# A two-block transformer kernel on one core: every modulation column is summed on TensorE, and the later columns move from the first projections into the attention slots

## The chip, the cores and the metric

The kernel runs on one core of a Trainium2 chip, as one program. The metric is the device time of the whole program in microseconds. Times of a run are given as a median over several executions; the profile is of one further execution.

## What is computed

Two transformer blocks follow each other on a sequence of 512 tokens with 1024 channels, in 32-bit floats. What matters here is the start of the first block:

```
cond = silu(c)
mod  = cond @ ada_w + ada_b                      # 6 x 1024 values
shift1, scale1, gate1, shift2, scale2, gate2 = mod
u    = rmsnorm(x, norm_mix) * (1 + scale1) + shift1
aq, ak, av, bq, bkv, biq, bik, biw, cq, ck, cv, g = split(u @ w_in)
merged = sigmoid(g) parts * (diff_attention @ w_br_a, dsa_attention @ w_br_b, moba_attention @ w_br_c)
x    = x + gate1 * (merged @ w_o)
u2   = rmsnorm(x, norm_mlp) * (1 + scale2) + shift2
x    = x + gate2 * (square(relu(u2 @ w_ff1)) @ w_ff2)
```

`mod` is a row vector times a 1024 x 6144 matrix. The kernel holds it as 48 columns of 128 values (`modc[:, m]`): columns 0 to 15 are shift1 and scale1, 16 to 23 gate1, 24 to 39 shift2 and scale2, 40 to 47 gate2. The second block (a convolution and state-space mixer, gated linear attention, two cross attentions, two more feed-forward parts) takes most of the time and isn't touched.

## The kernel before, in words

**Units and slots.** Nearly all work with weights is cut into units. `plan` (L203) makes them and puts them in one fixed order. A unit is 128 output columns of a weight matrix: a 1024 x 128 block, 512 KB (`Unit`, L173). Every engine walks through the same order of units with its own function, and semaphores join them. SyncE (`sync_program`, L635) issues one transfer per unit into a ring of five slots (`RAW_SLOTS`, w0 to w4); before the transfer of unit n it waits until unit n - 5 has been used up (L644 to L655). A projection unit is split: ScalarE rounds the block to its high part (`round_ahead`, L1230, instruction L1239), VectorE or, for some units, GpSimd takes the low part (`lower_ahead`, L1796 and L2556), and TensorE makes 24 matmuls of 512 columns (`products`, L690, instructions L699, L701, L703). Both look up to four units or two split units ahead. "Slots" of an attention are the places at which each engine runs a few units between the scores of one tile and the rows of the tile before it. An attention has 16 tiles (4 heads x 4 query tiles) and 17 slots.

**Modulation units.** A modulation unit (name "ada") isn't split. Before the change there are two ways to use it. On VectorE (`ada_sum`, L1899): multiply the first 128-row chunk by its cond values (L1906), then multiply and add seven more (L1909), into one of two tiles `adat`; then TensorE adds over the partitions with one matmul against a column of ones (L740 in the opening, `ada_total` L721 and instruction L725 later), and VectorE adds the bias (L1915). On TensorE (`ada_first`, L729): eight matmuls, each with a 128 x 128 chunk as the stationary operand and one column of cond as the moving one (L737); the profile counts each 32-bit matmul as two instructions, so 16 for a unit.

**Order of the work around the change.**
- Opening (up to about 90 us): transposes of the input, then 12 "flips" for the bias tables (`flip_over`, L825, instruction L829; their operands come by GpSimd's transfers of 256 KB each, L2621, four ahead), with modulation units 0 to 15 between them: four ahead of head 1, then one for each head ahead of the flip of the head before. Even units go by VectorE, odd ones by TensorE. Then the first norm (`modulated`, L1986 and L1425) makes the inputs XH and XL.
- First projections (`plans["project"]`, 12 units): av, aq, ak. From the fourth on each is followed by a modulation unit (16 to 24), on VectorE.
- Differential attention, 17 slots: 15 projection units (cv, bq, kv, iq, ik, iw, cq, ck) and 17 modulation units (25 to 41), on VectorE. At the end of each head come the weighted values (`weigh`, L862, instruction L865) after ScalarE's copy of the transposed rows (L1228 in `rows_turned`, L1443), and a norm (L781).
- Index scores, 6 slots, and moba attention, 17 slots: gate and branch units only; the 48 selection rounds of VectorE (L2118, L2120) stand in moba's slots.
- Latent attention ("dsa"), 17 slots: gate and branch units, and modulation units 42 to 47 in the first six, with a last step "ada end".
- Then branch b, w_o, the feed-forward part, and the second block.

A few lines say how slots are filled before the change:

```
plans["project"] = project[:3]
for u in project[3:]:
    plans["project"] += [u, next(rest)]
for i in range(17):
    plans["diff", i] = [u for u in (next(fill, None), next(rest)) if u]
for i in range(6):
    plans["index", i] = [next(fill)]
```

## Time and profile before

| | |
|---|---|
| median of 3 runs | 3233.36 us (3229.53 to 3238.36) |
| the profiled execution, its own time | 3232.45 us |
| its span in the trace | 3230.7 us |
| busy: TensorE matmul, weight load | 2762.0 us (85%), 2164.7 us (67%) |
| busy: VectorE, ScalarE, GpSimd | 1678.0 us (52%), 1059.7 us (33%), 473.8 us (15%) |
| chain that ended last | TensorE 65%, VectorE 23%, ScalarE 7%, transfers 2% |
| VectorE, L1909 (sums of modulation units) | 280 instructions, 115.9 us, mean 414 ns |
| modulation weights | 48 transfers of 512 KB, 4.8 us to landing |

PE is TensorE's matmuls, PEld its weight loads, DVE VectorE, ACT ScalarE, POOL GpSimd, SP SyncE. Times count from the start of the span. "L699" is line 699 of the kernel. In a row of waits the engine and line that waited stand first, then what released it. A granted clock of 1.00 is 2.4 GHz and of 0.50 is 1.2 GHz. "ps" is an accumulator bank, "w_f" a weight slot, "modc" the modulation columns, "wh" and "w_r" high and low parts of a unit.

### The profile page before, as it was taken

The numbers are of one execution on the slowest core, as the hardware profiler recorded it, in microseconds if no ns is written. First come the engines' busy times: TensorE is split into PE (matmuls) and PEld (weight loads), VectorE is DVE, ScalarE is ACT, GpSimd is POOL, SyncE is SP. The second block draws the span as 40 slices with busy tenths as digits, with TensorE's granted clock in tenths as the row PEclk, the third lists the DMA queues.
The fourth block names the chain that finished last, engine by engine and source line by source line (L and its number), as shares of the span: only waits on it lengthen the run. The fifth ranks groups of instructions, "written<-read, shape, count | busy, mean of one in ns | idle before, by whom it ended". The sixth has DMA issues, their size and how long they took to land.

```text
span 3230.7 us, 29906 instructions
## 1 busy us (share of the span) xinstructions
PE 2762.0 (85%) x11897; PEld 2164.7 (67%) x11897; DVE 1678.0 (52%) x2474; ACT 1059.7 (33%) x1670; POOL 473.8 (15%) x344
## 2 busy tenths in 40 slices
PE   6879596889999987855669998999889899989996
PEld 5656364667888865644547866888657778668885
DVE  3466567545433259878865445332463373453324
ACT  2223342433332121221243434332343244343322
POOL 1021131320000024222311001000100030110001
PEclk6887797999999988977789999999999999999998
DMA  6442221222333321200023312333222033223331
GB/s 197 113 111 73 59 65 31 79 83 80 98 91 98 92 65 52 72 13 13 20 66 104 105 56 74 92 98 91 73 65 66 27 111 98 65 73 92 98 92 59
DMA packets 481275, 251.07 MB, mean 78 GB/s; under 512 B 13534, under 2 KB 478002, under 8 KB 481135
## 3 DMA queue, kind: packets, MB, share of 16 engines
q1 hardware_dynamic: 478516, 242.43, 26.3%
q0 software_dynamic: 1904, 5.73, 0.6%
q8 instruction: 93, 1.52, 0.2%
q10 hardware_dynamic: 715, 1.01, 0.1%
q14 instruction: 47, 0.39, 0.0%
HBM read 247.00 MB, written 2.13 MB: 77 GB/s over the span
## 4 chain that ended last, share of the span: by engine, by line
PE 65%; DVE 23%; ACT 7%; issue 2%; DMA 2%; POOL 0%; SPq 0%; DVEq 0%; ACTq 0%; POOLq 0%
PE ps L701 18%; PE ps L703 18%; PE ps L699 18%; DVE arena_f L2213 6%; DVE adat L1909 2%; DMA w_f<-in_w_in 2%; PE ps L865 1%; ACT wh L1239 1%; PE ps L1108 1%; PE ps L781 1%; DVE arena_f L1871 1%; ACT arena_f L1441 1%; DVE hT L2343 1%; DVE arena_f L1868 1%; ACT hT L1679 1%
## 5 line engine op out<-in xcount | busy, mean ns | idle before, releaser
L699 PE MATMUL ps<-XH,wh 128*128 128x512 f32 x2160 | 887.7, 411 | 81.8 <-ACT wh L1239 27.9
L703 PE MATMUL ps<-XH,w_r 128*128 128x512 f32 x2160 | 873.1, 404 | 21.5 <-POOL w_r L2556 12.2
L701 PE MATMUL ps<-XL,wh 128*128 128x512 f32 x1968 | 800.8, 407 | 3.9 <-DVE XL L1801 3.9
L1796 DVE TENSOR_TENSOR w_r<-w_f,wh 128x1024 fp32r<-128x1024 f32 x336 | 411.0, 1226 | 575.1 <-ACT wh L1239 575.0
L699 PEld LDWEIGHTS ps<-XH,wh 128*128 128x128 f32 x2160 | 421.9, 195 | 206.4 <-ACT XH L1665 30.2
L1239 ACT ACTIVATE wh<-w_f 128x1024 fp32r<-128x1024 f32 (+2 forms) x423 | 428.2, 1016 | 389.8 <-PE ps L703 310.7
L703 PEld LDWEIGHTS ps<-XH,w_r 128*128 128x128 f32 x2160 | 418.3, 194 | 127.4 <-POOL w_r L2556 18.7
L701 PE MATMUL ps<-arena_r,wh 128*128 128x512 f32 (+1 forms) x1280 | 479.9, 375 | 0.0
L701 PEld LDWEIGHTS ps<-XL,wh 128*128 128x128 f32 x1968 | 383.8, 195 | 97.6 <-DVE XL L1801 7.3
L699 PE MATMUL ps<-arena_r,wh 128*128 128x512 f32 (+1 forms) x944 | 351.9, 373 | 5.8 <-DVE hT L1844 3.1
L703 PE MATMUL ps<-arena_r,w_r 128*128 128x512 f32 (+1 forms) x944 | 345.7, 366 | 6.8 <-DVE w_r L1796 6.7
L2556 POOL TENSOR_TENSOR w_r<-w_f,wh 128x1024 fp32r<-128x1024 f32 (+3 forms) x87 | 187.8, 2163 | 791.3 <-ACT wh L1239 791.0
L701 PEld LDWEIGHTS ps<-arena_r,wh 128*128 128x128 f32 x1280 | 243.4, 190 | 45.4 <-issue 1.9
L2213 DVE SCALAR_TENSOR_TENSOR arena_f<-arena_f,vec 128x512 f32<-128x512 f32 x240 | 210.1, 875 | 8.5
L699 PEld LDWEIGHTS ps<-arena_r,wh 128*128 128x128 f32 x944 | 180.5, 191 | 44.2 <-issue 5.4
L703 PEld LDWEIGHTS ps<-arena_r,w_r 128*128 128x128 f32 x944 | 180.3, 191 | 37.9 <-DVE w_r L1796 8.1
L1228 ACT ACTIVATE arena_f<-ps 128x512 f32<-128x512 f32 (+4 forms) x188 | 87.5, 482 | 203.5 <-PE ps L703 97.9
L1325 ACT ACTIVATE arena_f<-ps 128x512 f32<-128x512 f32 x96 | 57.3, 597 | 275.0 <-PE ps L703 274.9
L2593 POOL TENSOR_TENSOR arena_f<-arena_f 128x512 f32<-128x512 f32 x48 | 50.0, 1042 | 554.3 <-ACT arena_f L1325 554.3
L1909 DVE SCALAR_TENSOR_TENSOR adat<-w_f,modc,adat 128x128 f32<-128x128 f32 x280 | 115.9, 414 | 9.9
L1272 ACT ACTIVATE sq<-hT 128x512 f32<-128x512 f32 x63 | 39.7, 632 | 213.5 <-DVE hT L1844 160.2
L1801 DVE TENSOR_TENSOR arena_r<-arena_f,arena_r 128x512 fp32r<-128x512 f32 x66 | 45.7, 693 | 119.4 <-ACT arena_r L1362 111.1
(302 smaller groups left out, 2838.6 us busy)
## 6 DMA issues: line engine op xcount, KB each, us to landing
w_f<-in_mlp_w SPq DMA_DIRECT2D x128, 512.0 KB, 3.9
w_f<-in_w_ff SPq DMA_DIRECT2D x64, 512.0 KB, 3.9
w_f<-in_w_in SPq DMA_DIRECT2D x49, 512.0 KB, 3.8
w_f<-in_ada_w SPq DMA_DIRECT2D x48, 512.0 KB, 4.8
w_f<-in_even_w_in SPq DMA_DIRECT2D x36, 512.0 KB, 3.8
w_f<-in_odd_w_in SPq DMA_DIRECT2D x24, 512.0 KB, 3.8
w_f<-in_even_w_out SPq DMA_DIRECT2D x16, 512.0 KB, 3.7
w_f<-in_xa_w_v SPq DMA_DIRECT2D x16, 512.0 KB, 3.5
```

The costliest lines, as they stand in the source:

```text
L699: e.matmul(b, hi[:, k, :], xh, start=u.first and k == 0, stop=False)
L701: e.matmul(b, hi[:, k, :], xl, start=False, stop=False)
L703: last = e.matmul(b, lo[:, k, :], xh, start=False, stop=u.final and k == u.kc - 1)
L1228: return e.activation(o, i, ACT.Copy, scale=scale).then_inc(act.sem, act.up(*mark))
L1239: e.activation(high_flat(u), flat(u, 0), ACT.Copy).then_inc(act.sem, act.up("high", u.n))
L1325: e.activation(ffn_h[:, m, :], b, ACT.Relu).then_inc(act.sem, act.up("ff relu", st, m))
L1796: e.tensor_tensor(flat(u, 1), flat(u, 0), high_flat(u).bitcast(F32), ALU.subtract).then_inc(dve.sem, dve.up("low", u.n))
L1801: e.tensor_tensor(o, i, high.bitcast(F32), ALU.subtract).then_inc(dve.sem, dve.up("xl", source, k))
L1909: e.scalar_tensor_tensor(out=a, in0=wt[:, k, :], scalar=cond[:, k, :], in1=a, op0=ALU.mult, op1=ALU.add).then_inc(dve.sem, dve.up("ada sum ...
L2213: e.scalar_tensor_tensor(out=o, in0=val[:, m, t:t + S], scalar=conv_tap(t, m), in1=o, op0=ALU.mult, op1=ALU.add).then_inc(dve.sem, dve.up())
L2556: e.tensor_tensor(flat(u, 1), flat(u, 0), high_flat(u).bitcast(F32), ALU.subtract).then_inc(pool.sem, pool.up("low", u.n))
L2593: e.tensor_tensor(ffn_h[:, m, :], ffn_h[:, m, :], ffn_h[:, m, :], ALU.mult).then_inc(pool.sem, pool.up("ffn", name[1], m))
```

## The change

All 48 modulation units are used on TensorE, by eight matmuls each. The VectorE sums, the two tiles `adat` and the products with ones are gone. In the opening TensorE writes columns 0 to 15 into one bank as before. For the later columns (`ada_block`) TensorE takes a bank of the attention's ring, and ScalarE adds the bias and writes the column. The first projections have no modulation units; the differential attention has units 16 to 32 in its 17 slots, the index scores 33 to 38 in 6, and the latent attention 39 to 47 in its first nine. SyncE's wait for a slot is always for TensorE. The diff:

```diff
--- before.py
+++ after.py
@@ -209,9 +209,7 @@
 
     project = (columns_of("av", w_in, COL_AV, 512, "X0", lead=True) + columns_of("aq", w_in, COL_AQ, 512, "X0")
                + columns_of("ak", w_in, COL_AK, 512, "X0"))
-    plans["project"] = project[:3]
-    for u in project[3:]:
-        plans["project"] += [u, next(rest)]
+    plans["project"] = project
 
     ik = Unit("ik", 0, [w_in[:, COL_IK:COL_IK + IDX_DIM]] * 4, "X0")
     iw = Unit("iw", 0, [w_in[:, COL_IW:COL_IW + 8]], "X0")
@@ -231,11 +229,10 @@
 
     fill = iter(branch(0, A["w_br_a"][0], "ya"))
     for i in range(6):
-        plans["index", i] = [next(fill)]
+        plans["index", i] = [next(fill), next(rest)]
     for i in range(17):
         plans["moba", i] = [u for u in (next(fill, None),) if u]
     fill = iter(branch(2, A["w_br_c"][0], "yc"))
-    rest = iter([*rest, Step("ada end")])
     for i in range(17):
         plans["dsa", i] = [u for u in (next(fill, None), next(rest, None)) if u]
     plans["branch b"] = branch(1, A["w_br_b"][0], "yb")
@@ -348,7 +345,6 @@
         XH = sb("XH", [P, KC, S], F32R)
         XL = sb("XL", [P, KC, S], F32R)
         high_slots = [sb(f"wh{i}", [P, KC, WC], F32R) for i in range(HIGH_SLOTS)]
-        adat = sb("adat", [P, 2, P])
 
         def two_views(name, words):
             start = -(-nc.sbuf_base // 32) * 32
@@ -409,7 +405,6 @@
             before = sq_rings[st] = Ring(f"sq {st}", [sq[:, 0, :], sq[:, 1, :]], rings, after=before)
         gate_ring = Ring("gates", [gates[:, j, :] for j in range(2)], rings)
         st_ring = Ring("soft", [soft[:, 4 * j:4 * j + 4] for j in range(8)], rings)
-        ada_ring = Ring("ada", [adat[:, j, :] for j in range(2)], rings)
 
 
         xin, o1 = area(0, NT, D)
@@ -644,10 +639,7 @@
             for u in units:
                 if u.n >= RAW_SLOTS:
                     old = units[u.n - RAW_SLOTS]
-                    if old.name == "ada" and not (old.m < 16 and old.m % 2):
-                        w.wait_ge(dve, "ada sum", old.m)
-                    else:
-                        w.wait_ge(pe, "unit", old.n)
+                    w.wait_ge(pe, "unit", old.n)
                 c = 0
                 for d in u.dram:
                     dst = chunks(raw_slots[u.raw][0], u.kc, u.cols)[:, :, c:c + d.shape[1]]
@@ -718,28 +710,19 @@
                         last = e.matmul(b[:, t * 8:t * 8 + 8], xh, lo[:, k, :], start=False, stop=k == KC - 1)
                 last.then_inc(pe.sem, pe.up("unit", u.n))
 
-            def ada_total(m):
-                b, freed = att_now[0].take("ada", m)
-                w.wait_ge(*freed)
-                w.wait_ge(dve, "ada sum", m)
-                e.matmul(b[:, 0:1], ada_ring.of(m), ones[:, 0:1], start=True, stop=True).then_inc(
-                    pe.sem, pe.up("ada", m))
-                ada_ring.free(pe, m)
-
-            def ada_first(u, b):
-
-                if u.m % 2 == 0:
-                    return
+            def ada_column(u, b):
+
                 wt = chunks(flat(u, 0), KC, P)
                 w.wait_ge(d_raw[u.raw], "unit", u.n)
                 w.wait_ge(dve, "cond")
                 for k in range(KC):
-                    last = e.matmul(b[:, u.m:u.m + 1], wt[:, k, :], cond[:, k, :], start=k == 0, stop=k == KC - 1)
+                    last = e.matmul(b, wt[:, k, :], cond[:, k, :], start=k == 0, stop=k == KC - 1)
                 last.then_inc(pe.sem, pe.up("unit", u.n))
-                w.wait_ge(dve, "ada sum", u.m - 1)
-                e.matmul(b[:, u.m - 1:u.m], ada_ring.of(u.m - 1), ones[:, 0:1], start=True, stop=True).then_inc(
-                    pe.sem, pe.up("ada", u.m - 1))
-                ada_ring.free(pe, u.m - 1)
+
+            def ada_block(u):
+                b, freed = att_now[0].take("ada", u.m)
+                w.wait_ge(*freed)
+                ada_column(u, b[:, 0:1])
 
             def memory_turn(li, k):
                 b, freed = att_now[0].take("mem", li, k)
@@ -756,13 +739,9 @@
                 while steps:
                     u = steps.pop(0)
                     if isinstance(u, Step):
-                        if u.name == "ada end":
-                            ada_total(47)
-                        else:
-                            memory_turn(u.name[1], u.m)
+                        memory_turn(u.name[1], u.m)
                     elif u.name == "ada":
-                        if u.m > 16:
-                            ada_total(u.m - 1)
+                        ada_block(u)
                     elif u.name == "iw":
                         index_weights(u)
                     else:
@@ -833,11 +812,13 @@
             w.wait_ge(*freed)
             for h in range(12):
                 for _ in range(4 if h == 0 else 1):
-                    ada_first(next(first), ada_bank)
+                    u = next(first)
+                    ada_column(u, ada_bank[:, u.m:u.m + 1])
                 if h:
                     flip_over(h - 1)
             flip_over(11)
-            ada_first(next(first), ada_bank)
+            u = next(first)
+            ada_column(u, ada_bank[:, u.m:u.m + 1])
             run("project")
             flush()
 
@@ -1289,7 +1270,15 @@
 
             def evacuate(u):
                 name, m = u.name, u.m
-                if not u.final or name in ("ada", "iw"):
+                if not u.final or name == "iw":
+                    return
+                if name == "ada":
+                    b = att_now[0].of("ada", m)
+                    w.wait_ge(pe, "unit", u.n)
+                    w.wait_ge(dve, "vec", 0)
+                    e.activation(modc[:, m:m + 1], b[:, 0:1], ACT.Identity, bias=column("ada_b", m)).then_inc(
+                        act.sem, act.up("mod", m))
+                    att_now[0].free(act, "ada", m)
                     return
                 b = lin.of(*u.out)[:, 0:u.tokens]
                 if name in copied:
@@ -1373,8 +1362,7 @@
                 while steps:
                     u = steps.pop(0)
                     if isinstance(u, Step):
-                        if u.name != "ada end":
-                            memory_part(u.name[1], u.m)
+                        memory_part(u.name[1], u.m)
                         continue
                     round_ahead(u.n)
                     evacuate(u)
@@ -1812,7 +1800,9 @@
                 name, m = u.name, u.m
                 if not u.final:
                     return
-                b = None if name == "ada" else lin.of(*u.out)
+                if name == "ada":
+                    return
+                b = lin.of(*u.out)
                 if name == "iw":
                     w.wait_ge(pe, "unit", u.n)
                     e.tensor_scalar(iw, b[:, 0:32].rearrange("p (a b) -> p a b", a=NT),
@@ -1831,7 +1821,7 @@
                 elif name in RESIDUAL:
                     st = RESIDUAL[name]
                     w.wait_ge(pe, "unit", u.n)
-                    w.wait_ge(dve, "mod", 47)
+                    w.wait_ge(act, "mod", 23 if st == "r0" else 47)
                     e.scalar_tensor_tensor(out=hT[:, m, :], in0=b[:, :], scalar=gate(0 if st == "r0" else 1, m),
                                            in1=hT[:, m, :], op0=ALU.mult, op1=ALU.add).then_inc(dve.sem, dve.up("h", st, m))
                     lin.free(dve, *u.out)
@@ -1896,25 +1886,6 @@
                     e.scalar_tensor_tensor(out=go[:, m, :], in0=sca[:, m % 2, :], scalar=1.0, in1=go[:, m, :],
                                            op0=ALU.add, op1=ALU.mult).then_inc(dve.sem, dve.up("og", m))
 
-            def ada_sum(u):
-
-                a, freed = ada_ring.take(u.m)
-                wt = chunks(flat(u, 0), KC, P)
-                w.wait_ge(*freed)
-                w.wait_ge(d_raw[u.raw], "unit", u.n)
-                w.wait_ge(dve, "cond")
-                e.tensor_scalar(a, wt[:, 0, :], cond[:, 0, :], None, ALU.mult).then_inc(dve.sem, dve.up())
-                for k in range(1, KC):
-                    w.wait_ge(dve, dve.count)
-                    e.scalar_tensor_tensor(out=a, in0=wt[:, k, :], scalar=cond[:, k, :], in1=a, op0=ALU.mult, op1=ALU.add).then_inc(
-                        dve.sem, dve.up("ada sum", u.m))
-
-            def ada_total(m):
-                b = att_now[0].of("ada", m)
-                w.wait_ge(pe, "ada", m)
-                e.tensor_tensor(modc[:, m:m + 1], b[:, 0:1], column("ada_b", m), ALU.add).then_inc(dve.sem, dve.up("mod", m))
-                att_now[0].free(dve, "ada", m)
-
             def memory_part(li, k):
                 b = att_now[0].of("mem", li, k)
                 w.wait_ge(act, "xh", ("mem", li), k)
@@ -1929,20 +1900,12 @@
                 while steps:
                     u = steps.pop(0)
                     if isinstance(u, Step):
-                        if u.name == "ada end":
-                            ada_total(47)
-                        else:
-                            memory_part(u.name[1], u.m)
+                        memory_part(u.name[1], u.m)
                         continue
-                    if u.name == "ada" and u.m > 16:
-                        ada_total(u.m - 1)
                     lower_ahead(u.n)
-                    if u.name == "ada":
-                        ada_sum(u)
-                    else:
-                        evacuate(u)
-                        if u.pair:
-                            evacuate(steps.pop(0))
+                    evacuate(u)
+                    if u.pair:
+                        evacuate(steps.pop(0))
 
             def run(stage):
                 run_steps(plans[stage])
@@ -1969,14 +1932,8 @@
                 add_square("mix", k)
             e.memset(lamb[BUCKETS:BUCKETS + 1, 0:12], 1.0).then_inc(dve.sem, dve.up("table row"))
 
-            def ada_first(u):
+            for u in plans["ada first"]:
                 lower_ahead(u.n)
-                if u.m % 2 == 0:
-                    ada_sum(u)
-
-            for u in plans["ada first"]:
-                ada_first(u)
-            w.wait_ge(pe, "ada", 14)
             w.wait_ge(pe, *unit_mark("ada", 15))
             e.tensor_tensor(modc[:, 0:16], lin.of("ada first")[:, 0:16], columns("ada_b", 0, 16), ALU.add).then_inc(
                 dve.sem, dve.up("mod", 15))
@@ -1987,6 +1944,8 @@
                 s = modc[:, 24 * i + 8:24 * i + 16]
                 ring = sq_rings[f"n{i}"]
                 w.wait_ge(dve, dve.count)
+                if i:
+                    w.wait_ge(act, "mod", 39)
                 e.scalar_tensor_tensor(out=s, in0=s, scalar=1.0, in1=columns(name, 0, 8), op0=ALU.add, op1=ALU.mult).then_inc(
                     dve.sem, dve.up("gain", i))
```

## Rows read from the trace of the kernel before

**Rows 1.** The page: granted TensorE clock in 40 equal slices, in tenths
```profile
...
PEclk6887797999999988977789999999999999999998
...
```

**Rows 2.** Windows: start:end length, busy us PE PEld DVE ACT POOL, clock, DMA share, GB/s
```profile
...
41.90:72.80 30.90, 30.87 (x90) 21.60 (x91) 6.14 (x18) 4.84 (x9) 4.83 (x9) 0.50 0.80 241
...
121.40:183.80 62.40, 48.94 (x189) 37.77 (x187) 26.88 (x71) 11.71 (x15) 2.39 (x1) 0.89 0.44 118
183.80:396.50 212.70, 159.79 (x625) 114.96 (x624) 132.13 (x318) 75.17 (x146) 37.44 (x17) 0.79 0.30 80
396.50:440.50 44.00, 40.27 (x156) 25.66 (x156) 19.66 (x28) 16.94 (x33) 13.08 (x9) 0.91 0.15 42
...
547.30:600.00 52.70, 40.87 (x170) 30.89 (x169) 35.30 (x84) 15.47 (x35) 15.21 (x12) 0.93 0.31 86
...
```

**Rows 3.** TensorE in order of time, opening (start us, duration, line, count, [idle before])
```profile
...
31.70 3.57 PE L737 MATMUL ps<-modc,w_f 128*128 128x1 f32 x16
...
41.93 2.07 PE L829 MATMUL ps<-arena_f,const 128*128 128x512 f32 x2 [2.40 <-DMA arena_f<-strip]
...
47.50 3.76 PE L829 MATMUL ps<-arena_f,const 128*128 128x512 f32 x4
51.05 3.41 PE L737 MATMUL ps<-modc,w_f 128*128 128x1 f32 x16
54.32 0.56 PE L740 MATMUL ps<-ones,adat 128*128 128x1 f32 x2
...
83.78 1.87 PE L737 MATMUL ps<-modc,w_f 128*128 128x1 f32 x16
87.26 0.59 PE L740 MATMUL ps<-ones,adat 128*128 128x1 f32 x2 [1.60 <-DVE adat L1909]
```

**Rows 4.** Chain of waits inside the first projections (start us, us, what)
```profile
...
127.67 3.86 DMA w_f<-in_w_in
...
131.56 1.07 ACT wh L1239
...
132.72 1.23 DVE w_r L1796
...
136.95 4.01 DMA w_f<-in_w_in
...
```

**Rows 5.** TensorE in order of time, first projections: one unit without a wait
```profile
...
115.79 0.48 PE L699 MATMUL ps<-XH,wh 128*128 128x512 f32 x1
...
121.43 0.28 PE L725 MATMUL ps<-ones,adat 128*128 128x1 f32 x2
...
```

**Rows 6.** TensorE's waits, first projections from 121.4 us (total us, times, longest)
```profile
...
PE ps L725 <- DVE adat L1909: 13.5, 6, 3.5
```

**Rows 7.** TensorE's waits, differential attention, 183.8 to 396.5 us
```profile
...
PE ps L725 <- DVE adat L1909: 16.8, 5, 7.8
...
PE ps L865 <- ACT arena_f L1228: 10.7, 3, 6.0
PE ps L850 <- ACT arena_f L1252: 4.2, 1, 4.2
...
PE ps L850 <- DVE arena_f L2036: 3.4, 3, 1.4
PE ps L865 <- DVE modc L1915: 2.6, 1, 2.6
```

**Rows 8.** TensorE's waits, latent attention's slots with a modulation column, 547.3 to 600 us
```profile
PE ps L725 <- DVE adat L1909: 6.7, 3, 4.6
PE ps L865 <- ACT arena_f L1228: 5.1, 1, 5.1
```

**Rows 9.** Windows: an idle gap and behind it; 8-column matmuls (L716 to L718)
```profile
...
133.80:136.90 3.10, 0.00 (x0) 0.00 (x0) 2.85 (x10) 0.00 (x0) 0.00 (x0) 1.00 0.00 0
138.50:141.40 2.90, 2.90 (x8) 2.28 (x7) 0.00 (x0) 0.42 (x1) 0.00 (x0) 0.50 1.11 303
298.70:315.00 16.30, 16.30 (x80) 16.30 (x80) 7.46 (x18) 2.43 (x5) 3.79 (x2) 0.51 0.13 33
...
```

## The prediction

> **What bounds the kernel now.** I read the granted clock over the whole span first, then windows by stage, then TensorE's and the chain's own order of time in the stages that the change touches, then TensorE's waits there. The whole-span clock [rows 1] shows that TensorE is granted less than full speed in the first fifth of the span and nearly full speed after it; the change lies within the first 650 us. The windows [rows 2] show what limits each stage. In the opening TensorE is busy 30.87 of 30.90 us at 0.50 of full clock: it is the bound, at the lower level (1.2 GHz). In the first projections from 121.4 us it is busy 48.9 of 62.4 us. The chain inside that stage shows why [rows 4]: a weight load lands in 3.86 us, ScalarE rounds it (1.07), VectorE takes the low part (1.23), then sums a modulation unit, and only that sum frees the slot for which the next load waits, 9.28 us later (127.67 to 136.95). A projection unit needs 5.64 us of TensorE when nothing is late (115.79 to 121.43) [rows 5]. So VectorE's sum sits in the loop of the loads. In the differential attention TensorE is busy 159.8 of 212.7 us; in the index scores 40.3 of 44.0; in the part of the latent attention with modulation columns 40.9 of 52.7 [rows 2]. TensorE's waits say what the idle time is made of [rows 6 to 8].
>
> **The price of a unit on TensorE.** A modulation unit on TensorE is 16 matmuls of one column. At 0.50 of the clock they take 3.27 us from start to the next instruction (51.05 to 54.32); the last such unit took 1.87 us [rows 3]. In the opening I take 3.27. In the attention slots the price p runs from 1.87 (full clock, no loss) to 3.27 plus the clock that such work costs its neighbours. Rows of that: behind a 3.10 us gap TensorE ran 2.90 us at the lower level, which loses 1.45 us of work; and 100 matmuls of 8 columns held it near 0.51 for 16.3 us while it was busy throughout [rows 9]. So p lies between 1.87 and 3.27 + 1.45 = 4.72. I take 2.5, nearer the lower end: between two modulation units there stands a projection unit of 5.64 us, long enough to win the clock back as it did behind the gap; about four such losses in ten units give 1.87 + 0.6.
>
> **Opening, +17.8 us.** Removed: 8 VectorE sums and 8 products with the ones column. Added: 8 units on TensorE, 16 in all. Flip 0 now starts at 41.93, when its transfer lands. Ahead of it come five units instead of two: 31.70 + 5 x 3.27 = 48.1, so that transfer is no longer the wait. Behind it are 12 flips at 1.78 us (47.50 to 51.05 for two) and 11 units: 48.1 + 21.4 + 36.0 = 105.5. Now it ends at 87.26 + 0.59 = 87.85, its two last waits for VectorE included [rows 3]. Rounded with the small gaps: +17.8. It delays the shift and gain columns of the first norm, and with them everything. Nearest upper bound the same; lower bound below, as a rival. The first projection loads move later with it, since their slots are freed by TensorE, but each has four units of lead.
>
> **First projections, -22.3.** Nine modulation units with their loads, sums and ones products leave. The 62.4 us from 121.4 to the first scores [rows 2] become 7 x 5.64 + 0.6 for the last transposes = 40.1. The waits are 13.5 of that [rows 6]; most of the rest is lower clock behind them. It needs the loads to keep up: a load is ready 3.86 + 1.07 + 1.23 = 6.2 us after its slot is free [rows 4], with five slots of 5.64 us each. If only the waits went, it would be -13.5; that is the bound on the other side.
>
> **Differential attention, 17p - 34.** It keeps 17 modulation units (now 16 to 32). VectorE loses 17 sums; TensorE gains 17p. TensorE's waits that go: 16.8 for the sums, 4.2 and 3.4 ahead of scores, and 8.3 of the 13.3 ahead of the weighted values (L865), where ScalarE's copy was held behind a load whose slot a VectorE sum freed late; what stays there is ScalarE's own copy, an estimated 1.25 us at each of four heads [rows 7]. That is 32.7; the 17 ones products give 2.4 back, and the last slot, which has no projection, keeps 1. The other waits (norms) remain. With p = 2.5: +8.5.
>
> **Index scores, 6p = +15.** Units 33 to 38, with six 512 KB loads on SP's queue, go into a stage where TensorE is busy 92% and transfers take a 0.15 share [rows 2]. Nothing there can hide TensorE work. The selection rounds behind it start later by the same amount; they stand in slots and don't absorb it.
>
> **Latent attention, 9p - 11.3 = +11.2.** Nine units instead of six. Waits that go: 6.7, and 3.8 of 5.1 [rows 8]; six ones products, 0.8.
>
> **At nothing.** ScalarE gets 32 additions of one column. None is in the trace; the nearest ScalarE row shown takes 1.07 us for 1024 columns [rows 4]. So they lie between 0 and 34 us in all; I take about 0.2 us each, hidden, because ScalarE's next step in every slot is the copy of transposed rows that TensorE makes after the modulation unit anyway. GpSimd's queue is not touched. SP waits for TensorE in place of VectorE: loads three units ahead wait for the modulation unit of the slot before, which is done before that slot's successor begins. The residual's wait on the last columns is long satisfied.
>
> **Sum.** 17.8 - 22.3 + 32p - 34 - 11.3 = 32p - 49.8. With p = 2.5: +30.2. The profiled execution took 3232.45 us, 0.9 below the median of the three runs, so no correction is needed: 3263. With p = 1.87 it is +10.0, with 3.27 +54.8. A gain would need p under 1.56 us, less than the fastest unit in the trace.
>
> **Rivals.** (1) Faster: **one-column products run at full clock**. The opening shows the reverse, 0.50 through 30.9 us of work without a gap [rows 2]. It would be supported only by the last unit of the opening at 1.87. Then the fifth unit ends at 31.70 + 9.35 = 41.05, before flip 0's transfer; with flips at an estimated 0.9 the opening ends at 41.93 + 10.8 + 20.6 = 73.3, -14.6; slots at 1.87 give 32p = 59.8; and the 0.79 clock of the attention [rows 2] would rise, an estimated 16 us. Sum: -14.6 - 22.3 + 59.8 - 45.3 - 16 = -38, 3194 us. It decides from the point at which the alternation of flips and units is granted the upper level. The Trainium skill, "TensorE: Matmul & The Clock Gate", section "What's actually happening", says that the throttled state is the default and activity releases it; by that rule the extra matmuls would warm the engine, while the opening's row says that this kind of activity does not. Chance 0.06.
> (2) No change: the opening is slow, but in the slots the gaps that cost the clock go, and p is 1.87: +10 less up to 16, so -6 to +9, about 3234. For it: six of ten gaps are VectorE's. Against: each unit is itself like a gap to the clock, by the 8-column row [rows 9]. Chance 0.15.
> (3) Worse: modulation units and the short projection units behind them (index, latent) keep TensorE at the lower level, p = 3.27 + 0.8: +80, 3313; or ScalarE waits at each load since the ring of five slots now holds only two and a half slots' units. For it: 0.15 DMA share is little, so mostly the clock. Chance 0.11.
> My forecast, p between 1.9 and 3.3: 0.68.
>
> **How the numbers follow.** A measurement of this kernel tells about 0.3%, 9.7 us, from no change. Forecast and rival 3 are slower (0.68 + 0.11); rival 2 is within; rival 1 faster. The range runs from 3235, which takes in much of rival 2, to 3292, beyond p = 3.27; outside are rival 1, a little of 2 and most of 3.
>
> **What would show it.** Right: an opening in which each unit takes TensorE 3.3 us and each flip 1.8, at 0.50 of the clock, up to about 105 us; first projections in units of 5.64 with no VectorE wait, first scores near 179 us; no wait of TensorE for a VectorE sum anywhere; the differential stage 5 to 15 us longer with clock near 0.8; index stage from 44 to about 59 us; everything after 680 us only shifted. Wrong: the opening ending before 90 us, units under 1.9 us on average, or the differential stage shorter than 205 us.

## The result and the profile after

The changed kernel took 3239.61 us (median of 14 runs, 3235.06 to 3245.72), the kernel before 3232.18 us on the same chips (14 runs, 3226.38 to 3238.61). The ratio is 1.0021, interval [1.0013, 1.003]: 0.2% slower, by the medians +7.4 us. That is within the 0.3% that the prediction called no change, so rival 2 came true and the forecast of +30 us did not. The range held it, because it reached down to 3235 to take in rival 2; the size was four times too large.

The profiled execution took 3235.42 us (before: 3232.45), its span 3233.7 (before: 3230.7). The stages of the two profiled executions, each bounded by the first matmul of the next one (first projection, first score of each attention, first matmul of the latent attention's output):

| stage, us | before | forecast | after |
|---|---|---|---|
| opening | 90.0 | +17.8 | 107.6 (+17.6) |
| first projections | 93.8 | -22.3 | 70.7 (-23.1) |
| differential attention | 212.7 | +8.5 | 204.2 (-8.5) |
| index scores | 43.9 | +15 | 61.5 (+17.6) |
| moba attention | 106.8 | 0 | 108.9 (+2.1) |
| latent attention | 111.7 | +11.2 | 108.2 (-3.5) |
| the rest | 2571.6 | 0 | 2572.5 (+0.9) |

From the page of the changed kernel, the busy times, the clock in 40 slices and the chain's shares:

```profile
PE 2832.1 (88%) x12457; PEld 2244.9 (69%) x12457; DVE 1540.5 (48%) x2122; ACT 1070.0 (33%) x1702; POOL 474.3 (15%) x344
...
PEclk6897787989999988976789999999999999999998
...
PE 73%; DVE 18%; ACT 6%; issue 2%; POOL 0%; DMA 0%; SPq 0%; DVEq 0%; ACTq 0%; POOLq 0%
```

TensorE has 70 us more work and VectorE 137.5 us less, and the span is nearly the same. The chain has moved from VectorE (23% to 18%) to TensorE (65% to 73%). The clock [rows 1] is lower in slice 6, in which the index scores now end, and higher in slice 3. Windows of the changed kernel, columns as in [rows 2]: opening behind the first unit, first projections, index scores, the latent attention's slots, and the differential attention:

```profile
31.40:105.00 73.60, 73.60 (x279) 61.21 (x278) 2.45 (x2) 10.41 (x17) 7.76 (x14) 0.51 0.54 152
107.60:178.30 70.70, 70.57 (x304) 56.55 (x304) 23.41 (x32) 24.75 (x35) 6.55 (x3) 0.98 0.33 87
382.50:444.10 61.60, 60.07 (x252) 43.74 (x252) 19.00 (x30) 18.68 (x38) 12.84 (x9) 0.80 0.27 75
...
553.10:651.30 98.20, 92.83 (x481) 75.03 (x480) 36.01 (x74) 43.42 (x98) 36.66 (x30) 0.99 0.36 98
...
178.30:382.50 204.20, 183.19 (x863) 143.11 (x862) 61.25 (x158) 80.22 (x162) 33.66 (x15) 0.83 0.30 82
```

In the opening TensorE is busy for all of 73.60 us at 0.51, the lower level (1.2 GHz). By the Trainium skill, "TensorE: Matmul & The Clock Gate", section "What's actually happening", the throttled state is the default and activity releases it. The opening here is 73.60 us without a gap, and nearly all of it isn't released, so this mix of work doesn't act as that rule would have it; the measurement decides. Only the last unit ran partly at the upper level (2.19 us), behind the last two flips, which stand in a row; e1 below shows the same unit and the same flips at the upper level in another order. In the projections TensorE now has no gap (70.57 of 70.70) and the clock is 0.98. In the differential attention TensorE has 23.4 us more work [rows 2] in 8.5 us less time.

TensorE in order of time, changed kernel, opening (L719 is the one-column matmuls, L808 the flips), and then one slot of the differential attention at full clock:

```profile
31.40 17.23 PE L719 MATMUL ps<-modc,w_f 128*128 128x1 f32 x80
48.49 2.05 PE L808 MATMUL ps<-arena_f,const 128*128 128x512 f32 x2
50.34 3.41 PE L719 MATMUL ps<-modc,w_f 128*128 128x1 f32 x16
53.61 2.05 PE L808 MATMUL ps<-arena_f,const 128*128 128x512 f32 x2
...
103.24 2.19 PE L719 MATMUL ps<-modc,w_f 128*128 128x1 f32 x16
107.61 0.77 PE L691 MATMUL ps<-XH,wh 128*128 128x512 f32 x1 [2.17 <-ACT XH L1416]
...
235.66 0.39 PE L691 MATMUL ps<-XH,wh 128*128 128x512 f32 x1
235.89 0.40 PE L693 MATMUL ps<-XL,wh 128*128 128x512 f32 x1
...
239.13 1.84 PE L719 MATMUL ps<-modc,w_f 128*128 128x1 f32 x16
240.83 0.30 PE L839 MATMUL ps<-const,arena_f 128*128 128x128 f32 x1
```

A unit takes 3.27 us in the opening (50.34 to 53.61), as before [rows 3], and 1.70 us from start to start in a slot (239.13 to 240.83). The 1.87 that the prediction took from [rows 3] as its lower bound was the busy time of one unit with its end; the next matmul starts before that end. This row carries most of what follows.

TensorE's waits of the changed kernel in the differential attention (first fence) and in the latent attention's slots (second), to be held against [rows 7, 8]:

```profile
PE ps L760 <- ACT stat L1249: 10.9, 5, 4.9
PE ps L879 <- DVE arena_f L2043: 3.6, 1, 3.6
PE ps L846 <- ACT arena_f L1209: 3.1, 4, 0.8
PE ps L839 <- DVE arena_f L2019: 2.7, 1, 2.7
```

```profile
PE ps L839 <- ACT arena_f L1209: 2.4, 1, 2.4
PE ps L846 <- ACT arena_f L1209: 2.3, 3, 0.9
```

Every wait for a VectorE sum is gone. The wait ahead of the weighted values (L865 before, L846 after) fell from 10.7 and 2.6 to 3.1 us, and in the latent attention the trace of before, read up to 649.1 us, had 17.9 us of waits where 4.7 are left. Of the kernel before, the window of that part and its two longest waits:

```profile
547.30:649.10 101.80, 83.12 (x352) 62.16 (x350) 57.10 (x129) 40.58 (x89) 37.28 (x30) 0.95 0.29 79
...
PE ps L865 <- ACT arena_f L1228: 6.9, 3, 5.1
PE ps L725 <- DVE adat L1909: 6.7, 3, 4.6
```

### The profile page after: what moved, and what is told of

Read it like the earlier page. It is cut to its first block, busy times and chain, and to the rows that moved or that the text cites. A ratio compares the mean times of both kernels' runs of the same rounds, so it can differ in the third digit from the quotient of the medians.

```text
span 3233.7 us, 30720 instructions
## 1 busy us (share of the span) xinstructions
PE 2832.1 (88%) x12457; PEld 2244.9 (69%) x12457; DVE 1540.5 (48%) x2122; ACT 1070.0 (33%) x1702; POOL 474.3 (15%) x344
## 3 DMA queue, kind: packets, MB, share of 16 engines
q1 hardware_dynamic: 478516, 242.43, 26.5%
## 4 chain that ended last, share of the span: by engine, by line
PE 73%; DVE 18%; ACT 6%; issue 2%; POOL 0%; DMA 0%; SPq 0%; DVEq 0%; ACTq 0%; POOLq 0%
PE ps L691 20%; PE ps L693 20%; PE ps L695 20%; DVE arena_f L2172 6%; PE ps L719 3%; PE ps L846 1%; PE ps L831 1%; PE ps L1089 1%; PE ps L760 1%; DVE arena_f L1861 1%; ACT wh L1220 1%; DVE hT L2302 1%; DVE arena_f L1858 1%; ACT hT L1667 1%; ACT arena_f L1209 1%
## 5 line engine op out<-in xcount | busy, mean ns | idle before, releaser
L719 PEld LDWEIGHTS ps<-modc,w_f 128*128 128x128 f32 x768 | 120.4, 241 | 15.0 <-issue 11.8
L719 PE MATMUL ps<-modc,w_f 128*128 128x1 f32 x768 | 115.0, 280 | 0.0
```

Of the source, the lines that this page charges most:

```text
L719: last = e.matmul(b, wt[:, k, :], cond[:, k, :], start=k == 0, stop=k == KC - 1)
```

## The experiments

Two theories stood at the start. **The additive one:** the stages change one by one, the opening and the index scores pay, the projections gain, and the two attentions come out near zero because a unit costs 1.70 us and the clock that it costs only replaces the clock that VectorE's gaps cost. **The one-sum rival:** the small total is one effect (the end is set elsewhere, by VectorE or the transfers), so undoing a part changes little. Where an expectation uses a letter, A is the additive reading with a unit that costs its own time alone; D and H are the readings in which the clock around the unit decides. The stages of every run's profiled execution, in us:

| run | opening | proj. | diff. | index | moba | latent | rest | median | ratio to before |
|---|---|---|---|---|---|---|---|---|---|
| before | 90.0 | 93.8 | 212.7 | 43.9 | 106.8 | 111.7 | 2571.6 | 3232.18 | |
| after | 107.6 | 70.7 | 204.2 | 61.5 | 108.9 | 108.2 | 2572.5 | 3239.61 | 1.0021 |
| e1_opening_split | 86.4 | 71.3 | 194.9 | 61.6 | 108.9 | 108.1 | 2572.1 | 3210.66 | 0.9942 |
| e2_opening_tensor_only | 107.6 | 95.5 | 215.9 | 44.4 | 107.1 | 112.1 | 2571.3 | 3249.60 | 1.0066 |
| e3_index_units_in_moba | 105.9 | 71.9 | 202.0 | 47.3 | 107.3 | 108.1 | 2571.9 | 3215.75 | 0.9960 |
| e4_both | 87.1 | 71.2 | 197.9 | 44.1 | 107.1 | 108.2 | 2571.1 | 3187.49 | 0.9877 |
| e5_doubled_in_diff | 106.3 | 71.9 | 267.0 | 60.2 | 107.3 | 108.3 | 2572.2 | 3295.92 | 1.0204 |
| e6_placement_only | 86.2 | 71.5 | 205.9 | 52.9 | 107.1 | 118.9 | 2571.7 | 3217.58 | 0.9968 |
| e7_engine_only | 85.5 | 87.9 | 195.9 | 42.8 | 106.1 | 101.6 | 2574.3 | 3199.73 | 0.9911 |
| e8_opening_vector | 90.6 | 71.1 | 197.2 | 42.8 | 107.9 | 108.1 | 2569.4 | 3199.51 | 0.9908 |
| e9_moba_and_latent | 88.3 | 71.1 | 197.2 | 42.8 | 130.0 | 91.4 | 2570.8 | 3193.66 | 0.9891 |
| e10_unit_inside_projection | 106.2 | 72.0 | 194.8 | 53.6 | 107.5 | 107.1 | 2577.2 | 3213.79 | 0.9957 |
| e11_inside_and_moba | 84.5 | 71.8 | 194.8 | 47.4 | 128.3 | 91.9 | 2574.0 | 3194.42 | 0.9895 |
| e12_best | 87.1 | 71.3 | 194.6 | 44.2 | 107.1 | 108.0 | 2575.1 | 3188.20 | 0.9869 |

Each interval is about 0.0015 to either side (0.0012 to 0.0022), some 5 us. A difference from the changed kernel is worked out from the two ratios, times 3230; two runs of few executions each are known against each other to some 7 us.

**e1: the opening split over both engines again.** Even units 0 to 14 go back to VectorE; all else is the changed kernel.

```diff
+                    if old.name == "ada" and old.m < 16 and old.m % 2 == 0:
+                        w.wait_ge(dve, "ada sum", old.m)
+            def ada_first(u, b):
+                if u.m % 2 == 0:
+                    return
+                ada_column(u, b[:, u.m:u.m + 1])
+                w.wait_ge(dve, "ada sum", u.m - 1)
+                e.matmul(b[:, u.m - 1:u.m], ada_ring.of(u.m - 1), ones[:, 0:1], ...)
```

> The changed kernel, but the opening's even units go by VectorE again, as before the change; the slots stay as changed. Theory A (the loss stands in two places, the opening with +17.6 us and the index scores with +17.6, and the differential and latent slots gain): the first projection starts near 90 instead of 107.6 us, and nothing later takes it back, so 7.4 - 17.6 = -10 against the kernel before, about 3222 us. Rival B (stage differences are absorbed by what follows, as a later stage waits for something else): the time stays within 4 us of the changed kernel, about +5.

Measured: 0.9942 [0.9927, 0.9956], 19 us faster than before and 26 us faster than the changed kernel. That is 9 more than theory A expected (-10 against before). The opening gives 21.2 of it (107.6 to 86.4), more than the 17.6 between the first two profiles. All eight profiles with the opening split lie from 84.5 to 90.0 us, of which 90.0 is the kernel before; the five with all of it on TensorE lie from 105.9 to 107.6. The means are 86.9 and 106.7, so the price of the whole opening on TensorE is about 20 us. TensorE in order of time in this kernel (L725 is a unit, L823 the flips):

```profile
59.72 3.76 PE L823 MATMUL ps<-arena_f,const 128*128 128x512 f32 x4
63.27 2.15 PE L725 MATMUL ps<-modc,w_f 128*128 128x1 f32 x16
...
65.50 1.96 PE L823 MATMUL ps<-arena_f,const 128*128 128x512 f32 x4
67.30 1.84 PE L725 MATMUL ps<-modc,w_f 128*128 128x1 f32 x16
```

In this order two flips stand in a row between the units, and behind such a pair the clock rose in the middle of the opening: a unit at 1.84 us and two flips in 1.80 (65.50 to 67.30) in place of 3.27 and 3.55. It didn't rise behind the pairs before that one. With a single flip between the units, as in the changed kernel, it didn't rise until the end. The two openings differ in the number of units too, so which of the two decides isn't shown.

The differential attention gives 9.3 more in the profile, though nothing in it was edited. Its window and its waits in this kernel:

```profile
157.70:352.60 194.90, 173.69 (x864) 136.56 (x862) 61.23 (x158) 80.36 (x162) 33.71 (x15) 0.87 0.32 86
```

```profile
PE ps L775 <- ACT stat L1262: 10.9, 5, 4.9
PE ps L892 <- DVE arena_f L2072: 3.6, 1, 3.6
PE ps L859 <- ACT arena_f L1222: 3.1, 4, 0.8
PE ps L852 <- DVE arena_f L2048: 2.8, 1, 2.8
```

Held against the changed kernel's rows, the instructions, the waits and the other engines' work are the same; only the clock differs, 0.87 for 0.83. Clock times length is 169.6 here and 169.5 there: the same work at another clock. It can be located: of the 14 projection units of the stage, which take 5.7 us each at full clock, five took 7.2 in the changed kernel (at 195.73, 206.07, 215.89, 308.81 and 318.61), and none did in e1, where one took 6.1. So the time of this stage moves by up to 9 us between profiled executions of the same instructions. e2 shows it too, with the stage as before: 215.9 for 212.7. **No stage difference under about 9 us in the differential attention, read from one profile, is evidence of anything by itself.** Medians of several runs are needed there, and the medians say -26 where the opening alone says -21. Whether this is chance or follows from the opening isn't shown. The kernels that make the same instructions in this stage read 204.2 and 202.0 (e3) behind a long opening and 194.9, 197.9 (e4), 197.2 (e8, e9) behind a shorter one, which speaks for a part that follows from it.

**e2: the opening on TensorE alone, the rest as before.** The 16 units of the opening as in the change, all other placements and engines as before. The edit is shown against the kernel before.

```diff
-                    if old.name == "ada" and not (old.m < 16 and old.m % 2):
+                    if old.name == "ada" and old.m >= 16:
                         w.wait_ge(dve, "ada sum", old.m)
-                if u.m % 2 == 0:
-                    return
...
-                w.wait_ge(dve, "ada sum", u.m - 1)
-                e.matmul(b[:, u.m - 1:u.m], ada_ring.of(u.m - 1), ones[:, 0:1], ...)
...
-                if u.m % 2 == 0:
-                    ada_sum(u)
```

> The kernel before with one part of the change: all 16 units of the opening on TensorE; the later units stay on VectorE and in their old places. Theory A: opening +17.6 and nothing else moves, so +17 to +18 us, about 3250. Rival B: VectorE, freed of eight sums, and the later start let loads run ahead, and less than +9 is left.

Measured: 1.0066 [1.0051, 1.008], +21 us; its opening is 107.6, as in the changed kernel. With e1 this shows the opening's term from both sides, near its forecast size. The additive theory holds, and the rival falls.

**e3: the six index units in moba's slots.**

```diff
-        plans["index", i] = [next(fill), next(rest)]
+        plans["index", i] = [next(fill)]
-        plans["moba", i] = [u for u in (next(fill, None),) if u]
+        plans["moba", i] = [u for u in (next(fill, None), next(rest) if 10 <= i < 16 else None) if u]
```

> The changed kernel, but units 33 to 38 stand in moba's slots 10 to 15, where there is no projection unit and TensorE waits 4 to 6 us for VectorE's selection rounds, instead of in the index scores. Theory A (a unit of 1.7 us on an engine without idle time is paid in full, and it costs clock besides): the index stage goes back from 61.6 to 44 us, the moba stage stays at 109, so about -17 against the changed kernel, -10 against the kernel before. Rival C (the index stage is longer because its loads and the accumulator ring are shared, and that goes with the units): moba's stage grows by about 10 us and only -7 against the changed kernel is left.

Measured: 0.996 [0.9948, 0.9973], 20 us under the changed kernel. The index stage falls from 61.5 to 47.3 and moba doesn't grow (108.9 to 107.3): where VectorE's selection rounds set the pace, six units on TensorE cost nothing. The index scores were the wrong place for them.

**e4: both edits.**

```diff
+ the edit of e1
+ the edit of e3
```

> Both edits together: the opening split as before, units 33 to 38 in moba's slots 10 to 15, units 16 to 32 and 39 to 47 on TensorE in the slots of the differential and latent attention. Theory A: the two add up, 7.4 - 17.6 - 17.6 = -28 against the kernel before, about 3204 us. Rival B: no more than the better one alone, -10.

Measured: 0.9877 [0.9861, 0.9893], 40 us under the kernel before and 46.5 under the changed one. e1 and e3 sum to 45.2 against the changed kernel, so the two are additive. Theory A had expected -28 against before; of the 12 us more, 9 are e1's surplus again.

**e5: each unit of the differential attention twice.** The eight matmuls run twice over; the second pass starts the sum anew, so the column's value stays the same.

```diff
-                for k in range(KC):
+                for k in [*range(KC)] * (2 if 16 <= u.m < 33 else 1):
```

> The changed kernel, with the eight matmuls of each of the 17 modulation units in the differential attention made twice (the second set starts the sum again, so the value is the same). It prices one more unit of one-column matmuls in a stage that is bound by TensorE. Theory A (16 instructions at the upper clock level, 1.70 us from start to start, with little clock lost around them): +29 us to +35 against the changed kernel. The price of my prediction, 2.5 us: +42. Rival D (one-column work counts for the clock like a gap, so that doubled blocks push the engine to the lower level around them): 3.3 us and more, +55 to +80.

Measured: 1.0204 [1.0182, 1.0226], +66 us against before and +59 against the changed kernel, 3.5 us for each of 17 added units, where the first copy had cost 1.70. The reading that a unit costs the same again (+29 to +35) falls, and so does the predicted price of 2.5 us (+42); the reading with the clock in it holds. Window and order of time of this kernel:

```profile
178.20:445.20 267.00, 248.62 (x1135) 198.34 (x1134) 61.23 (x158) 80.99 (x162) 34.05 (x15) 0.72 0.23 63
```

```profile
184.30 3.94 PE L719 MATMUL ps<-modc,w_f 128*128 128x1 f32 x32
188.16 1.22 PE L831 MATMUL ps<-arena_f 64*128 64x256 f32 x4
189.32 0.79 PE L691 MATMUL ps<-XH,wh 128*128 128x512 f32 x1
189.91 0.63 PE L693 MATMUL ps<-XL,wh 128*128 128x512 f32 x1
190.34 0.63 PE L695 MATMUL ps<-XH,w_r 128*128 128x512 f32 x1
```

The doubled unit at 184.30 still runs near full clock (3.86 us for two), but the projection unit behind it pays: its matmuls stand 0.43 us apart (190.34 less 189.91) where the full clock has them 0.23 apart (235.66 to 235.89 in the changed kernel). Over the whole stage TensorE's busy time grows by 65.4 us (183.19 to 248.62): 41.5 in the units themselves (28.9 would be 17 at 1.70), 12.2 in the projection units, and the rest in scores, transposes, weighted values and sums, whose instructions are the same. So the price of one-column work is its own time and a lower clock for itself and its neighbours. The second part was 1.8 us for each unit added here (3.5 less 1.70).

**e6: placement alone.** The places of the change, but all of before's VectorE sums and products with ones. The edit is shown against the kernel before.

```diff
-    plans["project"] = project[:3]
-    for u in project[3:]:
-        plans["project"] += [u, next(rest)]
+    plans["project"] = project
...
-        plans["index", i] = [next(fill)]
+        plans["index", i] = [next(fill), next(rest)]
```

> The kernel before with only the new places: no modulation units in the first projections, 17 in the differential attention (16 to 32), 6 in the index scores, 9 in the latent attention, all on VectorE as before; the opening as before. Theory A (the projections gain because the VectorE sum leaves the loop of the loads, whichever engine does it later): projections from 93.8 to about 71 us (-23); differential unchanged at 213; index +1 to +3, since VectorE waits there anyway; latent +3. Together -16 to -20. Rival E (the projections gain because TensorE took the units over, and units on VectorE in the index scores hold up its chain): index +15 as well, together -5.

Measured: 0.9968 [0.9956, 0.998], -10 us by the medians (-16.5 between the two profiles). The projections gain as much as in the change (71.5 for 93.8): that gain is of the place, whichever engine sums. But the index scores cost 9.0 more, between theory A's +1 to +3 and rival E's +15, and the latent attention 7.2 more. The two readings together expected -16 to -20 and -5, and neither came. In both stages an engine waits for a modulation column: VectorE 11.7 us in the index scores, TensorE 8.7 in the latent attention. Waits of this kernel, first VectorE's in the index scores, then TensorE's in the differential attention:

```profile
DVE modc L1913 <- PE ps L723: 11.7, 3, 7.1
```

```profile
PE ps L723 <- DVE adat L1907: 17.1, 5, 8.7
...
PE ps L863 <- ACT arena_f L1226: 8.8, 3, 5.1
```

**e7: engine alone.** The opening split and the places as before, from unit 16 on TensorE and ScalarE.

```diff
-    plans["project"] = project
+    plans["project"] = project[:3]
+    for u in project[3:]:
+        plans["project"] += [u, next(rest)]
...
-        plans["index", i] = [next(fill), next(rest)]
+        plans["index", i] = [next(fill)]
+            (the opening of e1)
```

> The changed engine in the old places: nine units in the first projections, 17 (25 to 41) in the differential attention, 6 in the latent attention, all on TensorE; opening as before. Theory A: projections 71 + 9 x 1.7 = 86 us instead of 93.8 (-8); differential -9 to -17 as in the changed kernel; index unchanged at 44; latent 111.7 - 3.5 - 3 x 1.7 = about 105 (-7). Together about -28 us. Rival F (the gain of the slots comes from the new places, not from the engine): no more than -10.

Measured: 0.9911 [0.9898, 0.9923], -29 us, as theory A expected (-28). The projections (87.9 for 93.8), the differential attention (195.9 for 212.7) and the latent attention (101.6 for 111.7) are shorter than before, and their TensorE waits for VectorE sums are gone. The opening's 85.5 for 90.0 is no part of the edit. Together with e6: the new engine pays in these three stages. It doesn't in the opening, and not in the index scores either, where six units cost 9.0 us on VectorE (e6) and 17.6 on TensorE. The new place pays in the projections and costs in the index scores with either engine.

**e8: the opening on VectorE alone,** otherwise e4. Units 1, 3, ... of the opening go by VectorE too.

```diff
+                for m in ([u.m - 1] if 0 < u.m < 15 else [14, 15] if u.m else []):
+                    w.wait_ge(dve, "ada sum", m)
+                    e.matmul(b[:, m:m + 1], ada_ring.of(m), ones[:, 0:1], ...)
```

> The version with split opening and units 33 to 38 in moba's idle slots, and all 16 units of the opening on VectorE. TensorE, at the lower clock level, then has only the 12 flips (1.8 us each) and 16 ones products; VectorE has 16 sums of 2.95 us = 47 us from 27.5 us on, and two low parts. Theory A (the opening is bound by TensorE at the lower level as long as it has units): VectorE becomes the bound, the first projection starts near 80 instead of 87 us, -7 against that version, -46 against the kernel before. Rival G (TensorE waits for each sum ahead of a flip, and the waits take the place of the units): no gain, or up to +5.

Measured: 0.9908 [0.9893, 0.9923], -30 us: 10 worse than the split of e4, where theory A expected 7 better. VectorE's order of time in the opening and TensorE's wait for it:

```profile
40.36 0.28 DVE L1907 TENSOR_SCALAR adat<-w_f,modc 128x128 f32<-128x128 f32 x1
40.67 2.67 DVE L1910 SCALAR_TENSOR_TENSOR adat<-w_f,modc,adat 128x128 f32<-128x128 f32 x7
43.26 0.28 DVE L1907 TENSOR_SCALAR adat<-w_f,modc 128x128 f32<-128x128 f32 x1
```

```profile
PE ps L731 <- DVE adat L1910: 28.9, 12, 9.5
```

A VectorE sum takes 2.90 us (40.36 to 43.26), and the opening has 16 of them besides VectorE's other work; now VectorE is late for TensorE by 28.9 us in all. Three of the flips ran at the upper level here (1.10 us each with the end, at 44.02, 46.55 and 49.46) and the later ones at the lower (2.05), so taking the units away didn't keep the clock up by itself. In the profile the opening is only 3.5 us longer than e4's, less than the split openings differ among themselves; its six executions lie from 3188.97 to 3204.0, and the profiled one is the shortest of them, so the rest of the 10 us isn't located.

**e9: the index units and the latent ones in moba,** otherwise e4: moba's slots 9 to 15 take two each and slot 16 one, 15 in all, and the latent attention has none.

```diff
-        plans["moba", i] = [u for u in (next(fill, None),) if u]
+        plans["moba", i] = [u for u in (next(fill, None), *([next(rest) for _ in range(2 if i < 16 else 1)] if i >= 9 else ())) if u]
```

> Split opening; units 16 to 32 on TensorE in the differential attention; units 33 to 47 in moba's slots 9 to 16, two each, where TensorE waits 26 us in all for the selection rounds; none in the index scores and none in the latent attention. Theory A (a unit costs nothing where TensorE waits, 1.7 us elsewhere): moba's stage stays at 107 us (15 units of 1.7 us = 25.5 in 26), latent from 108 to about 108 - 9 x 1.7 = 93, so -15 against the version with six units in moba (-40 against the kernel before): -55. Rival J (the loads and ScalarE's step for each unit hold up the rows of moba): moba's stage grows by the same 10 to 15 us.

Measured: 0.9891 [0.9876, 0.9906], -35 us, so 4.5 us slower than e4 and the same within the error, where theory A, from the free time of moba, expected -55. The latent attention gave back 16.8 and moba took 22.9. Windows of this kernel and of e4 in moba's last slots, and a pair of units of this one:

```profile
455.00:529.40 74.40, 73.03 (x305) 60.38 (x304) 39.46 (x88) 17.85 (x47) 3.07 (x2) 0.56 0.36 103
```

```profile
455.00:507.00 52.00, 43.21 (x163) 30.63 (x162) 39.52 (x90) 14.40 (x38) 3.07 (x2) 0.62 0.24 66
```

```profile
474.53 6.99 PE L725 MATMUL ps<-modc,w_f 128*128 128x1 f32 x32
481.38 0.88 PE L852 MATMUL ps<-const,arena_f 128*128 128x128 f32 x3
```

TensorE had 8.8 us free (52.0 less 43.21) and the clock was already at 0.62. Two units took 6.85 us, 3.4 each as in the opening. These slots have no projection unit in them; the one pair that stands right behind a projection unit (at 458.69) took 4.57. Rival J laid moba's growth to the loads and ScalarE's step, but TensorE's only listed wait in this stage is 3.0 us for ScalarE's copies. VectorE has the same 39.5 us in both; TensorE became the bound (73.03 of 74.40).

**e10: the unit in the middle of a projection unit,** otherwise the changed kernel: its 16 matmuls stand behind the first half of the projection unit's chunks, for eight chunks between the fourth and the fifth.

```diff
-            def products(us):
+            def products(us, between=None):
+                    if between and k == us[0].kc // 2:
+                        ada_block(between)
```

> The changed kernel; where a projection unit stands before a modulation unit, TensorE makes the 16 one-column matmuls in the middle of the projection unit and not behind it, so the stretch of small matmuls between two projection units is 1.7 us shorter. Work and places are otherwise the same. Theory H (what a unit costs beyond its 1.7 us is clock, and it is lost when unit, transposes and scores stand together as one stretch of about 3 us or more): no 7.4 us projection units in the differential attention (5 of 14 in the changed kernel), index scores from 61.6 to about 55 us, together -12 to -20 against the changed kernel, about -8 against the kernel before. Rival I (the clock is lost by the sum of small work, wherever it stands): within 5 us of the changed kernel.

Measured: 0.9957 [0.9944, 0.9969], 21 us under the changed kernel, just beyond theory H's -12 to -20. The index scores show it best, window of this kernel:

```profile
372.90:426.50 53.60, 51.41 (x253) 36.38 (x253) 17.64 (x28) 18.58 (x39) 12.85 (x9) 0.95 0.30 84
```

The same work as in the changed kernel's index window, at 0.95 instead of 0.80, 8.0 us shorter; e1, with the changed kernel's order, had 61.6 like it. What is left over 43.9 is 9.7, six units of 1.6. So the index stage's 17.6 were 10 of the units' own time and 8 of clock, and the clock's part hangs on where the unit stands. The differential attention read 194.8 as well, but e1 read 194.9 without this edit, so that is no evidence. Of the 21 us, 8 are thus shown. The length of about 3 us that theory H names isn't shown: in the changed kernel a unit and what stood behind it before the next projection unit took 3.1 us where that unit then ran 7.2 us (202.97 to 206.07), and as long where it ran 5.7 (247.61 to 250.72).

**e11: e10 with e9's places and the split opening.**

```diff
+ the edits of e9 and e10
```

> The two last edits together: moba's slots 9 to 16 hold units 33 to 47, and in the differential attention each unit stands inside the projection unit before it. Theories A and H: -55 and another 4 to 9 us for the projection units that keep the upper level, about -62 against the kernel before. Rival: nothing beyond -55.

Measured: 0.9895 [0.9881, 0.9908], -34 us: equal to e9, so the rival holds and not the -62. Moba stays at 128.3; its late slots have no projection unit to stand in.

**e12: e4 with the unit inside the projection.**

```diff
+ the edits of e4 and e10
```

> The version with split opening and one unit in each of moba's slots 10 to 15 (-40 us), and in the differential and latent attention each unit stands inside the projection or branch unit before it. The stage times of the runs so far: opening 87, projections 71, differential 195 (instead of 198), index 44, moba 107, latent 107, rest 2571: a span of about 3182 us. Theory H: -43 to -48 against the kernel before. Rival: no difference from -40, since only about two projection units per execution still lose the clock there.

Measured: 0.9869 [0.9852, 0.9887], 3188.20 us, -42 us, at the edge between the rival (-40) and theory H (-43 to -48). Against e4 the difference is 2.6 us, inside the interval: the order within a slot isn't shown to matter once the index units are gone. e4 and e12 beat both kernels by over 1%.

## Why the prediction was right in three stages and wrong in the two attentions

**Bounds of the kernel: right.** VectorE's sum sat in the loop of the projections' loads, and the opening was TensorE's at the lower level.

**Opening, +17.8: right, by its own steps.** 17.6 between the two profiles, +21 by the medians of e2, about 20 over all profiles (see e1). The first five units ended at 48.6 (forecast 48.1), each pair of flip and unit took 5.12 us (forecast 1.78 + 3.27), the last unit ended at 105.4 (forecast 105.5).

**First projections, -22.3: right.** -23.1, the first score at 178.33 (forecast 179). e6 shows that it is the placement that gives it.

**Index scores, +15: right in size, by the wrong split.** +17.6; e10 shows 10 of own time and 8 of lower clock.

**Differential attention, 17p - 34 = +8.5, and latent attention, 9p - 11.3 = +11.2: wrong.** They measured -8.5 and -3.5. The step that failed is "The price of a unit on TensorE", the term p = 2.5; the waits removed were sized well in the differential attention (32.7 forecast, 31.9 gone). Two parts of it:
- The lower bound 1.87 was a busy time and not the distance to the next instruction, which is 1.70. With p = 1.70 the prediction's own sum 32p - 49.8 is +4.6; measured are +3.0 in the profile and +7.4 by the medians.
- The 0.6 on top, "about four such losses in ten units", held in one stage only. Put back into the prediction's formulas, the measured stages give p = (34 - 8.5) / 17 = 1.5 in the differential attention, 17.6 / 6 = 2.9 in the index scores, and (11.3 - 3.5) / 9 = 0.9 in the latent attention. In the two attentions the waits that the units replace had cost clock too, and the clock came out higher: 0.79 to 0.83 in one, 0.95 (547.3 to 649.1 us before) to 0.99 in the other. TensorE's busy time says how much: it grew by 23.4 us in the differential attention where 17 units at 1.70 less 2.4 for the products with ones make 26.5, and by 9.7 in the latent attention (83.12 to 92.83) where nine less 0.8 make 14.5. In the index scores no wait was there to be replaced: 0.91 to 0.80. With VectorE's sums in their place (e6) it was 0.80 too, though the stage grew by 9.0 us only. The prediction charged the new clock loss everywhere and credited the old one nowhere but in a rival.

The two attentions measured 17.0 and 14.7 us less than forecast; +2.6 in the index scores, +2.1 in moba and +0.9 in the rest don't make up for it. That the total still lies in the range and on the side of the forecast is owed to the width of the range and to luck.

In the latent attention the prediction also read the waits only up to 600 us; up to 649.1 there were 17.9, of which 13.2 went. Nine units at 1.70 less 13.2 and less 0.8 for the products with ones make +1.3; the other 4.8 to the measured -3.5 are what the busy time gained by the clock.

The prediction named 1.87, the nearest row at full clock, as one end and gave rival 2 just this case ("the gaps that cost the clock go"), with a chance of 0.15. What it held against it, the 8-column row [rows 9], was right for slots like moba's (e9) and for two units in a row (e5), and wrong for one unit beside a projection unit in the two attentions. Its own mark, "the differential stage shorter than 205 us", fell on the wrong side at 204.2, and with the same instructions e1 read 194.9, further on that side. Two of its readings aren't in the rows as given: the row of 8-column matmuls has 80 instructions, not 100, and no row has six of ten gaps for VectorE; neither enters the sum.

**Rival 1** (one-column work at full clock) fell in the opening of the changed kernel, 0.51 through 73.60 us, and held in the slots, 1.70 a unit. e1, with half the units and the flips in pairs, was granted the upper level within its opening, so the one-column products alone don't decide it. **Rival 3** didn't come: the additions on ScalarE took 0.26 us each (L1279, 32 of them, forecast 0.2) and the changed kernel's TensorE has no listed wait for one of them. With units in moba's slots it has: 3.2 and 2.3 us in all in e3, 2.9 and 2.3 in e4, 4.8 and 2.3 in e12, the longest 2.5. They stand in free time there, since moba's stage didn't grow.

**Left open.** Of the 9 us by which the differential attention differs between the same instructions, the trace shows which projection units lost the clock and not why those. Of e10's 21 us, 13 aren't located. That medians give the change +7.4 and the profile +3.0 is of the size of that spread. Whether an order of the all-TensorE opening with the flips in a row would have the clock rise earlier, as in e1, wasn't tried.

## What to carry to other kernels

Before moving work to the engine that is the bound, price it from start to start and not by its busy time, and price it per stage: what the moved work costs in clock must be set against what the waits that it removes had cost in clock. Put such filler inside dense work (e10) or where another engine sets the pace (moba's slots took six units for nothing, and fifteen for 22.9 us), and keep an opening that is bound by TensorE shared with the idle VectorE. A change that sums to nothing can hold parts of +18, -23 and +18: undoing the two that cost gave the 1.2 to 1.3% that the whole had hidden (e4, e12).

## What the runs showed of the hardware

- 80 one-column matmul instructions in a row and then their alternation with 512-column flips kept TensorE busy for 73.60 of 73.60 us at a granted 0.51. A unit took 3.27 us there and 1.70 us beside projection units. With half the units and two flips in a row between them (e1) the clock rose within the opening: a unit then took 1.84 us and two flips 1.80.
- The same instructions with the same waits took 204.2 us at 0.83 and 194.9 us at 0.87, with a start 20.6 us apart; the 14 projection units make up 7.3 us of it (five at 7.2 us instead of 5.7, against one at 6.1).
- The same index work took 61.6 us at 0.80 with the one-column unit ahead of the scores and 53.6 us at 0.95 with it in the middle of the 512-column matmuls.
- Two units in a row in each slot (e5) took 3.86 us where one takes 1.70, and the 512-column matmuls behind them stood 0.43 us apart in place of 0.23. In all, an added unit cost 3.5 us.
- Six units in the index scores cost 9.0 us summed on VectorE (e6) and 17.6 us on TensorE.
